# Streaming the second feature block of each weight unit in even and odd groups

## The reference

```python
q, k, v = jnp.split(h @ w_in, [DA_QK, 2 * DA_QK], axis=-1)
...
u = jnp.square(jax.nn.relu(h @ w_up[i])) @ w_down[i]
...
h = h + jax.nn.sigmoid(h @ w_ple_gate[i]) * (p[i] @ w_ple[i])
...
proj = h @ w_in[l]
...
up = h @ ffn_w_up[l]
...
x = x + (jax.nn.gelu(gate) * val) @ ffn_w_down[l]
```

## Time and profile before

| what | value |
|---|---|
| median of 2 runs | 3540.6 us (3539.72 to 3541.49) |
| profiled execution, its own time | 3541.19 us |
| its span, first to last instruction | 3539.4 us |
| mean granted TensorE clock | 0.998 of full speed |
| TensorE matmul busy | 3501.5 us, 99% of the span |
| TensorE weight load busy | 2956.1 us, 84% |
| VectorE, ScalarE, GpSimd busy | 50%, 27%, 18% |

### The profile page before, as it was taken

The page is one execution under the profiler, slowest core; times in us unless marked ns, Lnnn a source line. Parts: engine busy times, 40 slices in busy tenths (PEclk is TensorE's granted clock), DMA queues, the critical chain, the costliest instruction groups (busy, mean ns, idle before and its releaser), DMA issues.

```text
span 3539.4 us, 44299 instructions
## 1 busy us (share of the span) xinstructions
PE 3501.5 (99%) x18416; PEld 2956.1 (84%) x18416; DVE 1769.1 (50%) x2276; ACT 960.5 (27%) x1679; POOL 633.1 (18%) x372
## 2 busy tenths in 40 slices
PE   9999999999999999999999999999999999999999
PEld 7788888889888888688888878888888888898887
DVE  5454334556653346763336455553474346563434
ACT  3562001334220013630113356210141215120102
POOL 2112111200031112031112111311121111211110
PEclk9999999999999999999999999999999999999999
DMA  5322222222122223122222221222222122322222
GB/s 206 108 74 94 95 95 94 103 85 85 65 103 98 95 84 111 60 90 95 95 97 94 101 84 72 98 96 95 84 80 99 72 95 95 107 96 95 96 95 72
DMA packets 65463, 332.88 MB, mean 94 GB/s; under 512 B 9795, under 2 KB 20291, under 8 KB 28532
## 3 DMA queue, kind: packets, MB, share of 16 engines
q1 hardware_dynamic: 44316, 303.50, 24.0%
q10 hardware_dynamic: 20952, 26.56, 2.3%
HBM read 326.22 MB, written 10.90 MB: 95 GB/s over the span
## 4 chain that ended last, share of the span: by engine, by line
PE 88%; DVE 6%; ACT 4%; issue 1%; POOL 1%; DMA 0%; DVEq 0%; ACTq 0%; POOLq 0%
PE proj L498 23%; PE proj L500 23%; PE proj L499 23%; PE proj L619 2%; PE proj L620 2%; PE proj L621 2%; PE proj L531 2%; PE proj L532 2%; PE proj L533 2%; DVE wlo L1768 1%; PE mix L709 1%; DVE s L1878 1%; ACT xh L1183 1%; ACT h L1186 1%; PE mix L735 1%
## 5 line engine op out<-in xcount | busy, mean ns | idle before, releaser
L468 POOL TENSOR_SCALAR whi<-raw 128x2048 fp32r<-128x2048 f32 x272 | 529.4, 1946 | 2676.3 <-DVE wlo L1768 1710.6
L498 PE MATMUL proj<-gh,whi 128*128 128x512 f32 x1952 | 775.3, 397 | 2.1 <-DVE wlo L1768 2.1
L500 PE MATMUL proj<-gh,wlo 128*128 128x512 f32 x1952 | 761.4, 390 | 0.0
L499 PE MATMUL proj<-gl,whi 128*128 128x512 f32 x1952 | 760.8, 390 | 0.0
L1768 DVE TENSOR_TENSOR wlo<-raw,whi 128x2048 fp32r<-128x2048 f32 x285 | 651.2, 2285 | 137.4 <-POOL whi L468 94.4
L498 PE MATMUL proj<-xh,whi 128*128 128x512 f32 x1760 | 692.8, 394 | 8.7 <-DVE wlo L1768 3.0
L500 PE MATMUL proj<-xh,wlo 128*128 128x512 f32 x1760 | 685.7, 390 | 0.0
L499 PE MATMUL proj<-xl,whi 128*128 128x512 f32 x1760 | 685.5, 389 | 0.0
L498 PEld LDWEIGHTS proj<-gh,whi 128*128 128x128 f32 x1952 | 367.0, 188 | 93.3 <-issue 15.6
L500 PEld LDWEIGHTS proj<-gh,wlo 128*128 128x128 f32 x1952 | 366.8, 188 | 77.5
L499 PEld LDWEIGHTS proj<-gl,whi 128*128 128x128 f32 x1952 | 367.1, 188 | 75.6 <-issue 1.9
(11 more groups left out here) (321 smaller groups left out, 4333.0 us busy)
## 6 DMA issues: line engine op xcount, KB each, us to landing
raw<-in_stream SPq DMA_DIRECT2D x286, 1024.0 KB, 4.8
da_b<-bias_da ACTq DMA_DIRECT2D x16, 512.0 KB, 3.4
bias_da<-bias_rows ACTq DMA_DIRECT2D x8, 512.0 KB, 8.7
h<-in_x ACTq DMA_DIRECT2D x4, 512.0 KB, 8.7
bias_sw<-bias_table ACTq DMA_DIRECT2D x1, 2048.0 KB, 9.9
pf<-in_p ACTq DMA_DIRECT2D x4, 512.0 KB, 6.8
sw_b<-bias_sw ACTq DMA_DIRECT2D x4, 512.0 KB, 4.4
out_features<-fin SPq DMA_DIRECT2D x8, 256.0 KB, 2.4
```

What stands on the lines that cost most here:

```text
L468: nc.gpsimd.tensor_scalar(whi[SLOT[n]][:, :, :], raw[SLOT[n]][:, :, :], 1.0, 0.0, ALU.mult, ALU.add).then_inc(hi_done, 1)
L498: nc.tensor.matmul(out, wh, ah, start=first, stop=False, skip_group_check=check)
L499: nc.tensor.matmul(out, wh, al, start=False, stop=False, skip_group_check=check)
L500: return nc.tensor.matmul(out, wl, ah, start=False, stop=last, skip_group_check=check)
```

## The change

The moving operand and the output of about half of the matmuls in the three helpers get another access pattern. `swapped` takes a stretch of columns as groups of `d`, numbered from 0, and goes first through the even groups, then through the odd ones. Input and output are taken in the same order, so each column still lands at its own place. `d` is 4, 8, 16 or 32 by the contraction block (`k % 4`). It is applied to feature block 1 in `feature_chunk` and `half_chunk`, and to token blocks 1 and 3 in `token_chunk`.

```diff
@@ -492,9 +492,15 @@
-            def passes(out, wparts, xparts, first, last, check=False):
+            def swapped(ap, k):
+
+                return ap.rearrange("p (a b d) -> p b a d", b=2, d=(4, 8, 16, 32)[k % 4])
+
+            def passes(out, wparts, xparts, first, last, check=False, order=None):
 
                 (wh, wl), (ah, al) = wparts, xparts
+                if order is not None:
+                    out, ah, al = swapped(out, order), swapped(ah, order), swapped(al, order)
                 nc.tensor.matmul(out, wh, ah, start=first, stop=False, skip_group_check=check)
...
-                                  (oh[:, k, :], ol[:, k, :]), k == 0, k == kn - 1)
+                                  (oh[:, k, :], ol[:, k, :]), k == 0, k == kn - 1, order=k if j else None)
...
+                    if st % 2:
+                        o, wh, wl = swapped(o, k), swapped(wh, k), swapped(wl, k)
...
+                    if j:
+                        o, ah, al = swapped(o, k), swapped(ah, k), swapped(al, k)
```

## The result

The changed kernel takes 3608.86 us (3608.19 to 3609.53) against 3540.6: 68 us more, a ratio of 1.0193 (95% interval 1.0149 to 1.0237). The prediction was 3541 in a range up to 3557.

A forecast was written before the change was run, and what follows sets the result against it. The prediction took TensorE's column streaming to bound the kernel. To the profiled 3541.2 us it added 0 for starting patterns, 0 for reads and 0 for writes, giving 3541 us, in a range of 3536 to 3557.

The forecast's parts named there:

- What bounds the kernel: TensorE, bound by the rate at which columns stream, so that extra matmul time goes to the end at full price.
- no instruction, wait or queue was touched: Claim that the change adds or removes no instructions or waits, passes no queue and alters no other engine's row.
- Decoding and starting a longer pattern: Cost of starting the 8064 swapped matmuls, put at 0 because the streaming of the matmul before hides it.
- The write side: Cost of writing outputs to PSUM in short runs, taken as 0; no row of the trace had such an output.
- rival of half pace on every swapped output: All 3.51 million swapped columns cost 0.40 ns more each: 1406 us, 4947 us in all; chance 0.03.
- The read side: Cost of reading the moving operand from SBUF over 417,000 runs: 8 us, with rounding 12, taken as 0.
- the likeliest case: No cost, or a cost inside the read bound of 12 us: 3537 to 3553 us; chance 0.82.
- a jump costs a column's time: Each run, on either side, loses one 0.42 ns period: 174 us, 3715 us in all; chance 0.08.
- Only groups of four: Only swapped matmuls with d = 4 stream at plain f32 pace: 359 us more, 3900 us; chance 0.03.
- The swap saves the fixed part: The 13 ns between matmuls vanish where swapped: 105 us saved, 3436 us; chance of faster 0.01.
- A price below 71 us: A visible slowdown of the swapped matmuls that stays under the 2% bound; chance 0.03.
- no reserve for a jump: Stated sign of error: a float32r stream at one column per period cannot absorb a jump, which half-paced rows can't tell.

The follow-up runs named there:

- d64: The changed kernel with groups of 64 in every contraction block; 3539.89 us, ratio 0.9999 to the kernel before.
- write_only: The changed kernel with only the output in swapped order and the moving operand read plainly; 3540.17 us, ratio 0.9998 to the kernel before.
- kinds: The kernel before with single swapped 512-column matmuls far apart in feature_chunk, in groups of 4 to 128; 3552.03 us, a single run without a ratio.
- d16: The changed kernel with groups of 16 in every contraction block; 3631.68 us, ratio 1.0261 to the kernel before.
- cut: The kernel before, nothing swapped, with one plain 512-column matmul of feature block 1 in contraction block 2 cut into two of 256; 3546.71 us, ratio 1.0017.

## Why the prediction was wrong

- What bounds the kernel: right. Nearly all that the 512-column stream lost went to the end: 70 us of longer distances became 67 of span. That no instruction, wait or queue was touched held too.
- Decoding and starting a longer pattern, taken as 0: right. `d64` and `write_only` have such patterns and cost nothing.
- The write side, taken as 0 from a row that jumps once: right, by `write_only`. The rival of half pace on every swapped output fell with it.
- The read side, taken as 0: this is the step that failed. It was read from `level`, whose plain f32 matmuls take 0.82 ns a column, and I wrote that a float32r stream at 0.42 might show what those rows hide. It did, yet all the cases with a price above that cap got 0.17 together, and I capped the likeliest case at 12 us by multiplying 0.02 ns a run from those rows. That cap had no ground: the rows were priced at another pace, and the changed kernel shows the read side at 0.16 ns a jump (68 us over 417,000), eight times as much, with no proportion to jumps at all.
- The rivals: "a jump costs a column's time" had the side right (reads) and the law wrong. `kinds` shows 3 ns of own price for 128 jumps (d = 4), 17 for 32 jumps (d = 16), 0 for 8 (d = 64). "Only groups of four" fell with `d16`, which is the slowest. "The swap saves the fixed part" fell for 512 columns.
- A price below 71 us was given 0.03, "as by a jump that stalls only now and then". The time fell into just this case.
- The model itself missed one thing. I took 227 ns as a cost of one matmul, the same whatever stands before it. It is the settled rhythm of an undisturbed stream. After most of the breaks seen here it takes one to ten matmuls at 224 to 237 ns to come back, by `kinds`, `cut` and the waits of the kernel before. The changed kernel disturbs it three times in six matmuls, so it never settles: the plain matmuls stand at 231.7, and a third of the loss is theirs. The evidence stood in the trace of the kernel before, around the first row from which I measured: three of the five distances of a tail lie just ahead of 1004.43 and two are among my 24 steps, which lifts their mean from 226.7 to 227.1 ns.
- The sign by which it was to be wrong, "no reserve for a jump", isn't what happened either: in `d64` each swapped 512-column matmul has eight runs and pays nothing, and the 256-column ones pay nothing even in groups of 4. Some reserve is there. How it is used up by shorter groups stays open.

## What to carry to other kernels

In a dense stream the cost of one matmul can't be read in isolation: look at the distances behind a break, too, and count breaks (another width, a wait, a jumping read) with their tails, here from nothing to 39 ns, and 25 behind a change of width. A pattern on the output side in groups of 4 to 64 floats was free, and on the moving side groups of 64 floats were; groups of 4 to 32 cost 13 to 45 ns for a single 512-column float32r matmul with its tail. The rows at half the pace gave no bound for the stream at full pace.

## What was not expected of the hardware

- The rhythm of 227 ns and its tail of 233 236 228 232 231 ns, the same after a narrower matmul and, but for the first values, after a swap. What sets it stays open. The tail's values repeat within 1 ns across runs and places, while the other engines and the transfers do different things beside it. Two windows of the kernel before with this tail (columns as in the earlier trace rows):

```profile
144.60:146.00 1.40, 1.40 (x9) 1.18 (x8) 0.79 (x5) 0.68 (x2) 1.23 (x1) 1.00 0.58 70
3157.00:3158.20 1.20, 1.20 (x8) 0.98 (x7) 1.20 (x1) 0.15 (x1) 0.00 (x0) 1.00 0.08 20
```

GpSimd is busy for 1.23 us in the first and not at all in the second, and the DMA engines for a share of 0.58 and of 0.08. This, and the two places with other weights, speak against those engines, the transfers and the weights' addresses as the cause. Whether the weight load beside each matmul has a part in it wasn't tested.
- The 13 ns over the columns' own time are no fixed cost. Where the granted clock is 0.50 (1.2 GHz), after 2.54 us without a matmul, the kernel before has no such part. Its window there, and its timeline:

```profile
944.60:946.80 2.20, 2.20 (x7) 1.72 (x6) 0.00 (x0) 0.00 (x0) 0.00 (x0) 0.50 0.00 0
```

```profile
943.99 0.76 PE L498 MATMUL proj<-xh,whi 128*128 128x512 f32 x1 [2.54 <-DVE xl L2168]
944.55 0.63 PE L499 MATMUL proj<-xl,whi 128*128 128x512 f32 x1
...
946.68 0.60 PE L498 MATMUL proj<-xh,whi 128*128 128x512 f32 x1
```

From 944.55 to 946.68 five distances in 2.13 us are 426 ns each, which is 512 periods of 1.2 GHz (426.7) and nothing more.

- Reads in groups of 4 or 8 make 256-column matmuls faster, 117.8 and 117.6 instead of 119.8 ns: what is a loss at 512 columns is a small gain at 256. Why the undisturbed distance is the longer one there wasn't settled.
- Why groups of 16 cost most for the swapped matmul itself (17 ns, against 3 at d = 4, 6 at d = 8, 9 at d = 32 and 0 at 64) is open as well. Every group starts at a multiple of `d`, and no run shifts them, so the part that the place of a group in SBUF may have isn't known either.
